# Mix product tile by tile, weight remainders on GpSimd, and the first expert indices in two halves

## The reference, cut to what matters

```python
mixed = jax.nn.sigmoid(gate_a) * y_a + jax.nn.sigmoid(gate_b) * y_b
h = h + mixed @ w_mix_out[l]                      # the mix product
h = h + peer_ffn(rmsnorm_2(h, norm2_g[l]), peer_w_q[l], peer_sub_keys[l], peer_u[l], peer_v[l])

def peer_ffn(x, w_q, sub_keys, expert_u, expert_v):   # per tile of 128 tokens, 8 heads
    qh = (x @ w_q).reshape(tc, 8, 2, 128)
    scores = einsum('thpc,hpnc->thpn', qh, sub_keys)
    s_top, i_top = top_k(scores, 16)              # per half of a head
    c_s, c_pos = top_k(all 16 x 16 sums, 16)      # 16 experts per token and head
    g = softmax(c_s)
    a = gelu(einsum('td,thkd->thk', x, expert_u[e_idx]))
    return einsum('thk,thkd->td', g * a, expert_v[e_idx])
```

## Time and profile before

| what | value |
|---|---|
| median of 3 runs (lowest, highest) | 1768.57 us (1766.87, 1769.54) |
| the profiled execution: its own time, its span | 1768.28 us, 1766.5 us |
| busy: TensorE, VectorE, ScalarE, GpSimd | 92%, 66%, 47%, 19% of the span |
| bytes moved: gathers, unit loads and the rest | 268.45 MB, 194.29 MB |
| chain that ended last: TensorE, DMA, VectorE | 67%, 20%, 5% |
| issue to landing, median: unit load, gather | 4.8 us, some 36 to 38 us |

### The profile page before, as it was taken

The page is one execution under the profiler, slowest core; times in us unless marked ns, Lnnn a source line. Parts: engine busy times, 40 slices in busy tenths (PEclk is TensorE's granted clock), DMA queues, the critical chain, the costliest instruction groups (busy, mean ns, idle before and its releaser), DMA issues.

```text
span 1766.5 us, 21281 instructions
## 1 busy us (share of the span) xinstructions
PE 1616.7 (92%) x8160; PEld 1188.3 (67%) x8160; DVE 1163.3 (66%) x2017; ACT 834.6 (47%) x1553; POOL 342.2 (19%) x368
## 2 busy tenths in 40 slices
PE   6999999999999999999989998899988788778786
PEld 5998898888899899888879997555522232223232
DVE  4748865666675786666655566778667677766754
ACT  4446635433455663533345644455444444444443
POOL 0100000000020000000040100445544344434430
PEclk9999999999999999999999999899999999999999
DMA  6543464555543445455544354999999999999996
GB/s 239 197 148 128 143 216 166 191 191 191 188 155 141 143 167 214 159 201 188 188 159 144 143 194 188 395 401 421 422 421 421 421 421 422 421 422 422 422 421 282
DMA packets 67061, 464.43 MB, mean 263 GB/s; under 512 B 7440, under 2 KB 9616, under 8 KB 11536
## 3 DMA queue, kind: packets, MB, share of 16 engines
q0 software_dynamic: 36864, 268.45, 36.6%
q1 hardware_dynamic: 29808, 194.29, 30.3%
q10 hardware_dynamic: 288, 0.33, 0.1%
HBM read 462.00 MB, written 1.05 MB: 262 GB/s over the span
## 4 chain that ended last, share of the span: by engine, by line
PE 67%; DMA 20%; DVE 5%; issue 4%; ACT 3%; POOL 1%; SPq 0%; POOLq 0%; ACTq 0%; DVEq 0%
PE acc L543 13%; PE acc L545 13%; PE acc L544 13%; DMA row_w_lo<-in_peer_uv,arena 7%; DMA row_xa<-in_peer_uv,arena 7%; PE att L568 5%; PE acc L1654 4%; DMA arena<-in_peer_uv,arena 4%; PE acc L1657 4%; PE acc L568 3%; PE att L569 3%; DMA row_xb<-in_peer_uv,arena 2%; PE acc L569 2%; DVE w_lo L539 1%; ACT w_hi L532 1%
## 5 line engine op out<-in xcount | busy, mean ns | idle before, releaser
L539 DVE TENSOR_TENSOR w_lo<-arena,w_hi 128x2048 fp32r<-128x2048 f32 x176 | 403.1, 2299 | 188.7 <-ACT w_hi L532 188.3
L532 ACT CAST w_hi<-arena 128x2048 fp32r<-128x2048 f32 x176 | 335.6, 1908 | 131.9 <-PE acc L545 101.2
L1776 ACT ACTIVATE arena<-arena 128x1 f32<-128x1 f32 x256 | 51.9, 203 | 311.1 <-DVE arena L2059 141.4
L2059 DVE SCALAR_TENSOR_TENSOR arena<-arena 128x1024 f32<-128x1024 f32 x114 | 139.4, 1223 | 83.3 <-DMA arena<-in_peer_uv,arena 83.3
L543 PE MATMUL acc<-xa,w_hi 128*128 128x256 f32 x672 | 193.3, 288 | 0.0
L544 PE MATMUL acc<-xa,w_lo 128*128 128x256 f32 x672 | 191.3, 285 | 0.0
L545 PE MATMUL acc<-xa,w_hi 128*128 128x256 f32 x672 | 191.2, 285 | 0.0
L1654 PE MATMUL acc<-arena,gate_raw 128*128 128x512 f32 x226 | 126.7, 643 | 45.8 <-ACT gate_raw L1786 45.7
L2225 POOL DMA_INDIRECT arena<-in_peer_uv,arena x114 | 124.0, 1087 | 159.0 <-PE acc L1657 145.0
L651 POOL TENSOR_TENSOR small<-small 128x1 f32<-128x1 f32 x15 | 6.7, 448 | 704.9 <-ACT arena L645 704.9
L568 PE MATMUL att<-xa,w_hi 128*128 128x512 f32 x384 | 136.0, 398 | 0.0
(11 more groups left out here) (293 smaller groups left out, 3509.9 us busy)
## 6 DMA issues: line engine op xcount, KB each, us to landing
arena<-in_units SPq DMA_DIRECT2D x176, 1024.0 KB, 4.8
arena<-in_bias SPq DMA_DIRECT2D x1, 2048.0 KB, 9.8
arena<-in_peer_uv,arena POOLq DMA_INDIRECT x114, 36.4
x_res<-in_x SPq DMA_DIRECT2D x2, 512.0 KB, 4.2
arena<-in_norm_mix_g SPq DMA_DIRECT2D x2, 512.0 KB, 6.8
arena<-in_norm_mlp_g SPq DMA_DIRECT2D x2, 512.0 KB, 6.8
arena<-in_norm_g SPq DMA_DIRECT2D x2, 512.0 KB, 5.8
arena<-in_final_norm_g SPq DMA_DIRECT2D x2, 512.0 KB, 6.5
```

The source lines that it names most:

```text
L532: nc.scalar.copy(w_hi[:, s, :], raw[HOME[g]]).then_inc(S["hi_ready"], 1)
L539: nc.vector.tensor_tensor(w_lo[:, s, :], raw[HOME[g]], w_hi[:, s, :].bitcast(F32), ALU.subtract).then_inc(S["lo_ready"], 1)
L2059: nc.vector.scalar_tensor_tensor(row, row, 1.0, hn[:, n // SLOTS, :], ALU.mult, ALU.mult, accum_out=dots[:, n:n + 1]).then_inc(S["rows_use ...
```

## The change

- **Order and slots.** The mix units are loaded and split in the order 0, 2, 1, 3. Unit 2 has its rounded and rest parts in an extra slot (`more_hi`, `more_lo`, in the area `bias` that the raw slots of pq 5 and pq 6 take later, which therefore load later). Units 2, 1 and 3 are multiplied for tile 0 first. Tile 1's share of them is put behind head 0's queries and scores of tile 0.
- **Who makes the rest.** The rest of mix units 2, 1 and 3 and of pq 1 is made by GpSimd (`split_lo_by_pool`, line 568 after), in front of the first gather in its program. GpSimd's tensor_tensor does it on 128x2048 elements.
- **The norm.** The peer norm's factor (one over the root mean square) no longer multiplies the tokens. Tokens times the norm's weights go straight to the transposes, half a tile at a time; the factor enters as `scale` of the softmax's Exp and of Gelu.
- **VectorE's order.** Routing head 0 now stands in front of adding the mix product of tile 1 to the stream. Its indices are made in two steps of eight. The rests of pq 2 and pq 3 stand both in front of the first item's dot.
- **Places.** One more: six from the start, the seventh at item 6 (raw slot of pq 2), the eighth at item 8 (pq 3). The sub-keys are loaded earlier. Gelu's table is loaded by an idle instruction ahead of item 0.

The diff, cut to its core:

```diff
-PLACES = 17
-OPEN_FROM = [0] * 5 + [5, 6, 20, 30, 40, 50] + [72] * 6
+PLACES = 18
+OPEN_FROM = [0] * 6 + [6, 8, 20, 30, 40, 50] + [72] * 6
...
-    u += [("mix", i, "T") for i in range(4)] + [("pq", i, "F") for i in range(8)]
+    u += [("mix", i, "T") for i in (0, 2, 1, 3)] + [("pq", i, "F") for i in range(8)]
...
+        def split_lo_by_pool(pool, u):
+            g = counts.unit(u)
+            s = SLOT[g]
+            hi, lo = (w_hi[:, s, :], w_lo[:, s, :]) if s < RING else (more_hi[s - RING], more_lo[s - RING])
+            pool.wait_ge(S["hi_ready"], g + 1)
+            pool.wait_ge(S["lo_ready"], g)
+            nc.gpsimd.tensor_tensor(lo, raw[HOME[g]], hi.bitcast(F32), ALU.subtract).then_inc(S["lo_ready"], 1)
```

TensorE's program:

```diff
+            def mix_first_tile():
+                mix_part(2, 0, range(4), True, False)
+                mix_part(1, 0, range(4), False, True).then_inc(S["tile_done"], mark("tile_done", ("mix", 0)))
+                mix_part(3, 0, range(2), False, False)
+                pe.wait_ge(S["keys_ready"], at("keys_ready", 3))
+                half_pe(pe, 0, 0)
+                mix_part(3, 0, range(2, 4), False, True).then_inc(S["tile_done"], mark("tile_done", ("mix", 1)))
...
+            def mix_second_tile():
+                mix_part(1, 1, range(1), False, False)
+                pe.wait_ge(S["lo_ready"], QUERY0 + 1)
+                queries_of(0, 0, range(4))
+                half_pe(pe, 0, 1)
+                queries_of(0, 1, range(4))
+                queries_of(0, 0, range(4, 8))
+                queries_of(0, 1, range(4, 6))
                 rank_half(0)
-                tile_pe(pe, "n2", 1)
+                queries_of(0, 1, range(6, 8))
+                mix_part(1, 1, range(1, 2), False, False)
                 rank_half(1)
+                done(mix_part(1, 1, range(2, 4), False, True), 1)
+                done(mix_part(2, 1, range(4), True, False), 2)
+                done(mix_part(3, 1, range(4), False, True), 3)
...
+            def other_tile_queries():
+                half_pe(pe, 1, 0)
+                half_pe(pe, 1, 1)
+                queries_of(1, 0, range(8))
+                queries_of(1, 1, range(8))
```

ScalarE's:

```diff
-                nc.scalar.activation(w, w, ACT.Exp, accum_out=wsum[:, g:g + 1]).then_inc(
+                nc.scalar.activation(w, w, ACT.Exp, scale=peer_rstd[:, t:t + 1], accum_out=wsum[:, g:g + 1]).then_inc(
...
-                nc.scalar.activation(d, d, ACT.Gelu).then_inc(S["gelu_ready"], 1)
+                nc.scalar.activation(d, d, ACT.Gelu, scale=peer_rstd[:, t:t + 1]).then_inc(S["gelu_ready"], 1)
```

VectorE's, and GpSimd's:

```diff
+            def mix_first_tile():
+                dve.wait_ge(S["lo_ready"], QUERY0)
+                split_lo(dve, at_unit2["pq", 0])
+                dve.wait_ge(S["tile_done"], at("tile_done", ("mix", 0)))
+                mix_add(0, 0)
+                half_dve(dve, 0, 0)
...
+            for i in (2, 1, 3):
+                split_lo_by_pool(pool, at_unit2["mix", i])
+            norm_pool(pool, "n2", 0)
+            split_lo_by_pool(pool, at_unit2["pq", 1])
```

More of the change, by code:

```diff
@@ L255 @@
 QUERY0 = DEPTH * NU + NU2 - P_HEADS
-SLOT = [g % RING for g in range(QUERY0 + 2)] + [(QUERY0 + h % 2) % RING for h in range(2, P_HEADS)]
+MIX0 = QUERY0 - 4
+SLOT = [g % RING for g in range(MIX0 + 1)] + [RING, (MIX0 + 1) % RING, (MIX0 + 2) % RING]
+SLOT += [(MIX0 + h % 2) % RING for h in range(P_HEADS)]
 USER = [max((v for v in range(g) if SLOT[v] == SLOT[g]), default=None) for g in range(len(SLOT))]
@@ L500, in sync_program @@
             for u, unit in enumerate(units2):
-                if unit == ("mix", 0, "T"):
+                if unit == ("ga2", 0, "F"):
+                    sp.wait_ge(S["hn_ready"], at("hn_ready", ("n1", TT - 1)))
+                    for h in range(HP):
+                        sp.dma_start(raw_keys[:, h, :], A["peer_sub_keys_2"][0, h // 2, h % 2]).then_inc(
+                            S["keys_loaded"], mark("keys_loaded", h, 16))
+                elif unit == ("mix", 0, "T"):
                     sp.wait_ge(S["pair_done"], at("pair_done", STEPS[-1]))
@@ L1662, in second_pe @@
                 fresh, late = scored_at(u), scored_at(u - 2)
[L1663 removed]
+                if (name, i) in (("va", 1), ("mix", 1), ("mix", 2), ("mix", 3)) or name == "pq":
                     continue
@@ L1830, in second_act @@
             split_hi(act, 2)
-            for u, (name, i, kind) in enumerate(units2[:at_unit2["pq", 0]]):
+            for u, (name, i, kind) in enumerate(units2[:at_unit2["mix", 0]]):
                 fresh, late = scored_at(u), scored_at(u - 2)
-                if 0 < u and (name, i) != ("mix", 3):
-                    split_hi(act, u + 2)
+                for v in splits_at(u):
+                    split_hi(act, v)
                 if late:
@@ L1860, in second_act @@
             split_hi(act, at_unit2["pq", 3])
+            nc.scalar.activation(small[:, 120:121], zero_all, ACT.Gelu)
             for n in range(ITEMS):
@@ L1958, in take @@
                                                 ALU.subtract).then_inc(S["y_lo"], mark("y_lo", i))
-                elif name == "mix" and i == 1:
-                    unit(name, i)
-                    for t in range(TT):
-                        mix_add(0, t)
             def mix_add(half, t):
@@ L2136, in second_dve @@
                     normalise(scored_at(u - 1)[1])
-                if 0 < u and (name, i) != ("mix", 3):
+                if 0 < u and (name, i) != ("yab", 3):
                     split_lo(dve, u + 2)
```

236 lines of the change are left out of this document (142 added, 94 removed).

## The result

The changed kernel takes 1786.67 us (median of 4 runs, 1784.75 to 1787.28) against 1768.70 of the kernel before in the same job: a ratio of 1.0104 with a 95% interval of [1.0092, 1.0117], so 18 us slower. The forecast was 1769.5, its range ended at 1777. The profiled execution has a span of 1785.2 us, 18.7 more than before.

The account below looks back on a forecast made before the run. The DMA gather stream was taken as the bound, starting steadily once item 0 passes TensorE. Row 7's start +3.1, thin stretch -2.1 and Gelu's factor +0.1 made +1.1 net on 1768.28, forecast 1769.5 us, range 1764 to 1777.

Parts of the forecast that it names:

- when item 0 has gone through TensorE: Gather stream: item 0 passing TensorE, not gather 0 leaving, sets the end; row 0 at 1123.2, 3.4 us later than before.
- the head start of the gathers: First gather 8.7 us earlier, at 1095.1, all used up by the dry stretch; the rival that it is kept had 0.08.
- A rest on GpSimd: Each 128x2048 rest on GpSimd was taken to last 4.6 us, with bounds of 3.8 and 5.9.
- the 1.95 us added once for the first of a row: Mix stage: the first of GpSimd's rests in a row was taken to last 1.95 us more.
- The rests end at 1064.7, 1069.3 and 1073.9.: Mix stage: GpSimd makes three mix rests in a row from 1058.1, 4.6 us each plus 1.95 once.
- the 2.3 us for half of the indices: Head 0's routing: forming eight of sixteen indices takes 2.3 us, so the first eight are ready at 1094.0.
- The case of 516.82 in the earlier trace: Cited for the dear rival: a VectorE rest of 2.29 us took 2.87 while GpSimd's products ran.
- GpSimd is dear: Rival, chance 0.33: GpSimd's rests take 5.9 us each, the last mix rest ends 3.9 later, total 1773.3 us.
- The figure of 4.5 us: The skill's table time for two-input elementwise work on GpSimd at 2048 float32, cited beside the 4.6 us estimate.
- so 1.2 GHz until 4.7 us after it started. I take the same.: Tile 1's queries: after the pause TensorE runs 20 passes at 0.223 us and 28 at 0.112, pq 0 done at 1108.3.
- +1.1: Net change forecast against the profiled 1768.28 us: the 8.7 us head start all used up by the dry stretch.
- Its term of -2.1 for a thin stretch: Gather stream: with eight places gather 18 goes out 6 us ahead of need, so 2.1 us of thin stream go.

Follow-up runs that it names:

- experiment 8: Experiment 6's kernel with rows 0 and 1 multiplied ahead of pq 1's queries, dots 0 to 2 among the rests: 1767.26 us, ratio 0.9997.
- experiment 9: Experiment 8's kernel with TensorE's pauses around tile 1's transposes filled by 14, 7 and 1 identity transposes: 1765.92 us, ratio 0.9988.
- experiment 10: Experiment 8's kernel with gathers 6 and 8 given the places of rows 0 and 1: 1766.52 us, ratio 0.9989.
- experiment 11: Experiment 8's kernel with both the filled pauses of experiment 9 and the places of experiment 10: 1766.06 us, ratio 0.9993.
- experiment 12: The kernel before, with only pq 1's rest moved to GpSimd: 1765.93 us, ratio 0.9989.
- experiment 14: Experiment 1's kernel with TensorE's pause filled by 52, 7 and 1 identity transposes: 1768.78 us, ratio 1.0008.
- experiment 15: Experiments 5 and 6 together (VectorE's rests), with TensorE's pauses filled by 14, 7 and 1 transposes: 1764.20 us, ratio 0.9978.
- experiment 7: Experiment 1's kernel with all sixteen indices formed at once, not the first eight ahead: 1771.78 us, ratio 1.0024.
- experiment 3: The changed kernel with each GpSimd rest split into eight instructions of 128x256: 1782.43 us, ratio 1.0079.
- Experiment 4: The changed kernel with 64 identity transposes ahead of tile 1's, filling part of TensorE's pause: 1785.31 us, ratio 1.0095.
- experiment 13: The changed kernel, rests still on GpSimd, with TensorE's pauses filled by 78, 7 and 1 transposes: 1778.64 us, ratio 1.0064.
- experiment 1: The changed kernel with all four rests (mix units 2, 1, 3 and pq 1) back on VectorE: 1774.97 us, ratio 1.0037.
- experiment 2: The changed kernel with only the three mix rests on VectorE, pq 1's kept on GpSimd: 1778.77 us, ratio 1.0058.
- experiment 5: Experiment 1's kernel with row 0's dot ahead of pq 3's rest on VectorE: 1770.58 us, ratio 1.0019.
- experiment 6: Experiment 1's kernel with tile 1's sums between the first and second eight indices: 1770.25 us, ratio 1.0013.

## Why the prediction was wrong

**What held.** In twelve of the seventeen profiles (before, after, and all experiments but 8 to 12) the end lies 641.6 to 643.1 us behind gather 7: before 1766.5 - 1123.83 = 642.7, after 642.5, experiment 14 643.1, experiment 15 642.4. So "when item 0 has gone through TensorE" was the right term, and the head start of the gathers is worth nothing here (experiments 7 and 14). It has a limit: in experiments 8 to 12, where gather 7 leaves at 1109.4 to 1116.1, the end lies 647.2 to 653.4 us behind it, so from there on an earlier item 0 isn't worth its length. A rest on GpSimd takes 4.55 to 4.62, as worked out; the 1.95 us added once for the first of a row didn't show (4.62, then 4.57 and 4.55). From pq 1's last pass to row 0 it takes 8.8 us, 9.1 in the forecast.

| us | first half's transposes | second scores | first eight indices | pq 0 done | pq 1 done | row 0 |
|---|---|---|---|---|---|---|
| forecast | 1078.0 | 1087.6 | 1094.0 | 1108.3 | 1114.1 | 1123.2 |
| after | 1081.8 | 1094.0 | 1103.9 | 1121.8 | 1129.9 | 1138.7 |
| late by | 3.8 | 6.4 | 9.9 | 13.5 | 15.8 | 15.5 |

**The step that failed first: "The rests end at 1064.7, 1069.3 and 1073.9."** It took GpSimd as an engine beside VectorE. They are not beside each other: VectorE's sum stood 3.4 and 4.4 us, ScalarE's rounded parts behind it came late, and the last rest ended at 1078.0. The same failed again in the 2.3 us for half of the indices, where the shift of eight integers stood 3.6 us. The case of 516.82 in the earlier trace rows misled me. VectorE's 2.87 there stands beside GpSimd instructions of 0.7 us, so a wait for one of them looks like a small slowdown; experiment 3 shows just that (1.16 for 0.69). The rival "GpSimd is dear" had the sign, but put the price on GpSimd's own duration, where there is none. The Trainium skill has this on another page than the one I weighed: SBUF — State Buffer, section "SBUF: two separate sides", says that the port pair which the two share is locked for a whole instruction and the other engine waits in full, and names VectorE's work of two SBUF inputs or in a two-port mode. The traces agree with that rule: 4.09 and 5.06 us for two inputs, nothing for an input in PSUM. The shift has one input and took 3.72; that it ran in a two-port mode no trace here shows. (The figure of 4.5 us that the prediction takes from the Trainium skill, GPSIMD Engine Reference, stands in section 3.1, Elementwise — side-by-side cycle accounting, and not in 4.1; the traces agree, with 4.55 to 4.62.)

**The second: "so 1.2 GHz until 4.7 us after it started. I take the same."** The 0.50 clock held from 1103.0, in the pause, to 1126.9, 15.5 us into tile 1's queries. One case before was no measure of how long it lasts. I should have kept open the case that all of pq 0's passes, and half of pq 1's, run at 0.21 us a pass. Experiment 4 nearly talked me out of this cause, since it filled most of the pause and gained 1.4. Experiments 9, 11, 13 and 14 left no pause, and in each the clock stayed full until tile 1's queries were done; in the ten profiles that kept the pause or a part of it (the changed kernel, experiments 1 to 8 and 10) it fell. Nor did the forecast have a low clock at 1080, where it was 0.50 for 6.8 us.

**Their shares.** Above the kernel before, in per cent with both causes, without VectorE's stand, without the pause, and with neither: 1.04, 0.37, 0.64, 0.08 (after, experiments 1, 13, 14). VectorE's stand is worth 0.67 or 0.56 of these, 10 to 12 us; the clock in tile 1's queries 0.40 or 0.29, 5 to 7 us. The two values of each differ by 0.11, or 1.9 us, which is what the low clock at 1080 cost by the profiles. That would belong to both, since it follows the wait for GpSimd's last rest and is absent in experiment 13's profile though the edit doesn't touch it; the intervals are too wide to prove it. The 0.08 left over are 1.4 us, with 0 just inside the interval. That the forecast's sum was +1.1 is luck and no agreement: it held 20 passes at the low clock, some 2.2 us, and rests of 4.6 us on GpSimd, and experiment 14 has neither.

**The sum.** Its term of -2.1 for a thin stretch did not show: from gather 7 to the end it is 642.5 against 642.7. The stretch of the earlier trace rows is gone, but the stream is thin at 1145 to 1155 instead (338 and 378 GB/s in two windows of 5 us, some 1.5 us lost). Two slips in it change nothing: 0.3 above 1769.4 is 1769.7 and not 1769.5, and 8.7 ahead of 1106.8 is 1098.1 and not 1097.8. The factor in Gelu costs 0.09 an item (0.29 for 0.20), hidden for all but the last.
